# Two narrow score products as plain 32-bit products, and a later place for two kinds of VectorE work, in a hybrid encoder step

## The reference, cut to what matters

```python
def attend_block(q_nope, q_pe, q_chunk, k_nope, k_pe, v, k_chunk):
    s = jnp.einsum("bqhd,bkhd->bhqk", q_nope, k_nope) + jnp.einsum("bqhr,bkr->bhqk", q_pe, k_pe)
    s = s.astype(jnp.float32) * SM_SCALE
    mask = k_chunk[None, :] <= q_chunk[:, None]
    s = jnp.where(mask[None, None], s, -1e30)
    w = jax.nn.softmax(s, axis=-1).astype(v.dtype)
    return jnp.einsum("bhqk,bkhd->bqhd", w, v)
```

## Time and profile before

| what | value |
|---|---|
| median of 3 runs | 2449.06 us (2448.76 to 2449.34) |
| the profiled execution | 2446.93 us, of which its span 2445.1 |
| TensorE busy / weight loads | 99% / 96% of the span |
| VectorE, ScalarE, GpSimd busy | 74%, 52%, 22% |
| granted TensorE clock | 0.999 of full |

### The profile page before, as it was taken

One profiled execution on the slowest core, in us unless ns is written; L12 is line 12 of the kernel. 1 busy time (PEld: TensorE's weight loads), 2 busy tenths in 40 slices (PEclk: granted clock), 3 DMA queues, 4 the chain that ended last, 5 costly groups with the idle time before them and its releaser, 6 DMA issues. The chain is left out here.

```text
span 2445.1 us, 44182 instructions
## 1 busy us (share of the span) xinstructions
PE 2427.2 (99%) x17358; PEld 2340.8 (96%) x17358; DVE 1806.5 (74%) x2893; ACT 1283.4 (52%) x2306; POOL 537.9 (22%) x513
## 2 busy tenths in 40 slices
PE   9999999999999999999999999999999999999998
PEld 9999977899999999999999999778999999999998
DVE  8677767778776677677686777687787766776676
ACT  5566355655554454455535763557455544554454
POOL 0024155200112211220201142552002112211212
PEclk9999999999999999999999999999999999999999
DMA  4232200453447634664731221005435456546655
GB/s 164 71 115 73 53 11 20 88 154 106 96 86 139 129 84 98 133 120 90 221 100 52 61 73 54 11 20 115 133 109 114 88 115 132 109 87 121 132 104 185
DMA packets 109740, 242.48 MB, mean 99 GB/s; under 512 B 15536, under 2 KB 18960, under 8 KB 109408
## 3 DMA queue, kind: packets, MB, share of 16 engines
q0 software_dynamic: 48512, 102.26, 23.3%
q1 hardware_dynamic: 60880, 137.37, 18.0%
q10 hardware_dynamic: 144, 0.04, 0.0%
HBM read 147.39 MB, written 94.29 MB: 99 GB/s over the span
## 5 line engine op out<-in xcount | busy, mean ns | idle before, releaser
L3270 DVE TENSOR_TENSOR wlo<-raw_all,whi 128x512 fp32r<-128x512 f32 (+1 forms) x420 | 270.6, 653 | 181.1 <-ACT whi L2308 178.6
L2308 ACT ACTIVATE whi<-raw_all 128x512 fp32r<-128x512 f32 (+1 forms) x420 | 248.6, 599 | 278.4 <-DVE raw_all L3403 88.0
L3792 POOL DMA_DIRECT2D x_scratch<-stage x224 | 200.0, 943 | 839.1 <-DVE stage L3413 694.0
L2361 ACT ACTIVATE stage<-ps 128x536 f32<-128x536 f32 (+1 forms) x224 | 135.5, 612 | 148.6 <-PE ps L1590 143.6
L3413 DVE TENSOR_TENSOR stage<-stage,ps 128x536 f32<-128x536 f32 (+1 forms) x168 | 118.9, 708 | 84.8 <-PE ps L1590 84.0
L2873 DVE TENSOR_REDUCE mxp<-ps 128x1 f32<-128x80 f32 (+10 forms) x376 | 137.1, 376 | 51.7 <-PE ps L1304 47.7
L1113 PE MATMUL ps<-xgh,whi 128*128 128x358 f32 (+1 forms) x720 | 157.2, 326 | 0.0
L1113 PE MATMUL ps<-xgl,whi 128*128 128x358 f32 (+1 forms) x720 | 156.6, 325 | 0.0
L1113 PE MATMUL ps<-xgh,wlo 128*128 128x358 f32 (+1 forms) x720 | 156.5, 325 | 0.0
L1738 ACT ACTIVATE whi<-raw_all 128x1024 fp32r<-128x1024 f32 (+3 forms) x64 | 58.1, 908 | 174.5 <-PE ps L1113 158.0
L1113 PEld LDWEIGHTS ps<-xgl,whi 128*128 128x128 f32 x720 | 124.0, 189 | 0.0
(11 more groups left out here) (948 smaller groups left out, 7799.7 us busy)
## 6 DMA issues: line engine op xcount, KB each, us to landing
raw_all<-in_wst SPq DMA_DIRECT2D x237, 256.0 KB, 3.4
raw_all<-in_wst SPq DMA_DIRECT2D x74, 512.0 KB, 3.6
x_scratch<-stage POOLq DMA_DIRECT2D x120, 268.0 KB, 6.1
x_scratch<-stage POOLq DMA_DIRECT2D x120, 264.0 KB, 6.0
xall<-x_scratch SPq DMA_DIRECT2D x32, 537.0 KB, 8.6
x_scratch<-xall POOLq DMA_DIRECT2D x24, 537.0 KB, 3.5
raw_all<-in_wst POOLq DMA_DIRECT2D x30, 256.0 KB, 5.5
xall<-in_xT SPq DMA_DIRECT2D x8, 537.0 KB, 8.4
```

What stands on the lines that cost most here:

```text
L2308: nc.scalar.activation(dst, src, ACT.Copy).then_inc(S["u_hi"], 1)
L2361: nc.scalar.activation(quarters(stage_of(L, g, i, n)[:, 0:N2]), src, ACT.Copy, scale=-1.0 if row else 1.0).then_inc(S["x_copy"], 1)
L3270: V.tensor_tensor(dst, src, hi.bitcast(F32), ALU.subtract).then_inc(S["u_lo"], 1)
L3792: pool.dma_start(x_scr[2 * i + row, :, a:b], stage_of(L, g, i, n)[:, 0:b - a], accum_op=ALU.add).then_inc(S[done], 16)
```

## The change

- The scores of pairs 11 and 16 are made by one fp32 product each instead of three fp32r passes. Its operands are `q_plain` (the last 96 queries) and `k_plain` (the last 256 keys), which VectorE puts together from high and low parts in each head (`plain_parts`, two TENSOR_TENSOR, at step `PLAIN_AT` = 8). TensorE waits for them by the semaphore `plain`, which takes the place of `v_one`.
- `INVERT_AT` goes from 10 to 14.
- The copy of the sums of bank 1 goes from step 12 to step 13 (`SUM_LAG`).

```diff
+SUM_LAG = [OUT_LAG, OUT_LAG + 1, OUT_LAG]
-INVERT_AT = 10
+INVERT_AT = 14
+PLAIN = [PAIRS.index(SAMPLE_PAIR), PAIRS.index(LAST_PAIR)]
+PLAIN_AT = 8
+        q_plain = place("q_plain", "E", 2144 * 4, 64 + DEC)
+        k_plain = place("k_plain", "E", 2144 * 4 + 4 * (64 + DEC), 2 * P)
...
-                        for j, (a, c) in enumerate(PASSES):
+                        if i in PLAIN:
+                            w("plain", 1 + h + 1)
+                            mm = nc.tensor.matmul(ps[:, gi % 3, 0:n], k_plain[rows, k0 - LAST_KEYS:k0 - LAST_KEYS + P], q_plain[rows, q0 - STREAM + 64:q0 - STREAM + 64 + n],
+                                                  start=True, stop=True)
+                        for j, (a, c) in enumerate(() if i in PLAIN else PASSES):
...
+                def plain_parts(h):
+
+                    e = h % 2
+                    rows = slice(0, ALL_ROWS[e])
+                    w("aug", 32 * (h + 1))
+                    w("aug_few", 32 * (h + 1))
+                    w("q_lo", h + 1)
+                    if h == 0:
+                        w("kslot_lo", 1)
+                    else:
+                        w("kslot_lo", 4)
+                        w("s", h * NP)
+                    qh, ql = (qs[e][part][rows, STREAM - 64:TOK].bitcast(F32) for part in range(2))
+                    kh, kl = (ks[e][part][rows, LAST_KEYS:LAST_KEYS + 2 * P].bitcast(F32) for part in range(2))
+                    V.tensor_tensor(q_plain[rows, :], qh, ql, ALU.add)
+                    V.tensor_tensor(k_plain[rows, :], kh, kl, ALU.add).then_inc(S["plain"], 1)
...
+                        if i == PLAIN_AT:
+                            plain_parts(h)
...
-                            hb, ib = divmod(h * NP + i - OUT_LAG - BANK_LAST[n_bank], NP)
+                            hb, ib = divmod(h * NP + i - SUM_LAG[n_bank] - BANK_LAST[n_bank], NP)
```

More of the change, by code:

```diff
@@ L674, in trunk @@
             ("qr_raw", 2), ("qn", 4), ("qr", 2), ("ra0", 16 * 4), ("ra1", 16 * 4),
-            ("y_sq", 4), ("y_sum", 3), ("y_n", 4), ("v_one", 1), ("v_ev", 10), ("kf", 4),
+            ("y_sq", 4), ("y_sum", 3), ("y_n", 4), ("plain", 1 + NH), ("v_ev", 10), ("kf", 4),
             ("kslot_hi", 3), ("kslot_lo", 4),
@@ L2022, in o_out @@
                     nc.scalar.activation(d[r, q0:q1], ps[0:64, O_BANKS[n], 0:q1 - q0], ACT.Copy).then_inc(S["o_ev"], 1)
-                w("v_one", 1)
+                w("plain", 1)
                 for t in range(10):
@@ L2826, in _ @@
                     V.memset(kf[j][:, 3 * KCH:KW], 0.0)
-                V.memset(v[:, :].rearrange("p (t d) -> p t d", d=65)[:, :, 64:65], 1.0).then_inc(S["v_one"], 1)
+                V.memset(v[:, :].rearrange("p (t d) -> p t d", d=65)[:, :, 64:65], 1.0).then_inc(S["plain"], 1)
                 split(28)
```

## The result

The changed kernel takes **2470.37 us** (median of 5 runs, 2465.69 to 2473.74) against 2448.76 for the kernel before in the same comparison (5 runs, 2446.83 to 2449.34): ratio 1.0089, 95% interval 1.0075 to 1.0103. That is 21.6 us slower. I had forecast slower, but by 4.8 us, and the time lies above the top of the range. The profiled execution has a span of 2467.4 us.

A forecast was written before the change was run, and what follows sets the result against it. TensorE, busy 99% of the span, was taken to bound the kernel. The terms -3.5 - 7.5 + 10.1 + 4.5 + 1.2 gave +4.8 on the median 2449.06, so 2453.9 us, range 2447.0 to 2460.5.

The forecast's parts named there:

- the shifts of the few queries: Heads 3, 5, 7: GpSimd's small DMAs queue behind the reciprocals' store, TensorE waits 1.7 us six times: +10.1 us.
- The products: Pairs 11 and 16 on TensorE: one plain fp32 product saves 0.11 us over three passes: -3.5 us in all.
- The fifth rival: Pairs 11 and 16: fp32 weights load at half pace, adding time instead of saving: +7.0, 2460.9 us; 3%.
- The transposes: Attention stage: TensorE's 14 waits for VectorE's gathered maxima go, as copy and reciprocal move behind the gathering: -7.5 us.
- The third rival: Heads 3, 5, 7: `few_shifts` lands in time, its wait hidden; fully hidden -5.3, 2443.8 us; 12%.
- The new sums against GpSimd: Heads 0 and 4: GpSimd's low parts hold up VectorE's sums at step 8, so TensorE's maxima product waits: +4.5 us.
- rivals 1 and 2: VectorE's sums: not held by GpSimd, 2449.4 us, 15%; or GpSimd gets between head 0's two sums, 2459.8 us, 15%.
- the row at 221.52: GpSimd took 4.14 us while VectorE's sums ran, read as one side keeping the other out over several instructions.
- Head 7: Sums stand behind `yb20l`, so the 32-column product starts 0.9 us late, 0.3 comes back, in each layer: +1.2 us.
- The fourth rival: Attention stage: the transposes still wait because the sums are longer than thought: +7.5, 2461.4 us; 5%.
- The third step of the sum: Heads 3, 5, 7: delayed small DMAs of `few_shifts` taken to land in 1.6 us (1.5 to 2.2): +10.1 us.
- the forecast's own range: Whole kernel: 2451.5 to 2458 us, from the ends of the landing and of the products; the forecast had 50%.

The follow-up runs named there:

- the placed products alone: Changed kernel with both VectorE moves undone, GpSimd's queue as before, sums of head 0 at step 5 and head 7 at step 7: 2448.14 us, ratio 0.9997.
- the kernels with the exchange: `few_shifts` DMAs ahead of the reciprocals' store: changed kernel 2447.94 us; also sums of heads 0, 7 earlier 2443.68, 2442.89; without plain products 2443.98, 2444.37.
- the first five experiments: Reciprocals at step 10, 2451.25 us; GpSimd queue order, 2447.94; both VectorE moves without plain products, 2463.97; plain products without moves, 2454.76; head 5's weights later, 2459.88.
- everything placed: Changed kernel with `few_shifts` DMAs ahead of the reciprocals' store, sums of head 0 at step 5 and head 7 at step 7: 2443.68 us, again 2442.89.
- moves and exchange alone: Kernel before with both VectorE moves and `few_shifts` DMAs ahead of the reciprocals' store, without plain products and sums: 2443.98 us, again 2444.37.
- the moves alone: Kernel before with reciprocals at step 14 and the copy of bank 1 a step later, pairs by three passes, no sums: 2463.97 us, ratio 1.0064.

## Why the prediction was wrong

The term that failed is the third, the shifts of the few queries: its mechanism is the one that ran, but it measured 16.3 us and not 10.1. And the sum had no term for what long waits do to TensorE's clock, without a reason given; below it is estimated at 8.4 us. Term by term:

**The products (-3.5): right, a little too much.** Pair 11 of head 2, from the product of V ahead of it; the kernel before, then the changed one:
```profile
352.19 0.41 PE L1358 MATMUL ps<-pd,v 128*65 128x128 f32 x2
```
```profile
355.03 0.41 PE L1365 MATMUL ps<-pd,v 128*65 128x128 f32 x2
355.28 0.31 PE L1384 MATMUL ps<-q_plain,k_plain 97*128 97x32 f32 x2
355.42 0.48 PE L1311 MATMUL ps<-koh,qo 128*128 128x512 f32 x1
```
The plain product takes 0.14 us where I reckoned 0.22 to 0.26, 0.20 less than the three passes. But the product of V ahead of it, of type fp32 in both kernels, now takes 0.25 from start to start, not 0.17. The weight loads (engine PEld) show both at once; the kernel before, then the changed one:
```profile
352.33 0.30 PEld L1376 LDWEIGHTS ps<-qe,keh 97*128 97x128 f32 x2
352.67 0.19 PEld L1304 LDWEIGHTS ps<-koh,qo 128*128 128x128 f32 x1
```
```profile
355.17 0.30 PEld L1384 LDWEIGHTS ps<-q_plain,k_plain 97*128 97x128 f32 x2
355.40 0.19 PEld L1311 LDWEIGHTS ps<-koh,qo 128*128 128x128 f32 x1
```
From the first load of the pair to the next product's load it is 0.34 us for three passes and 0.23 for the plain product: two loads instead of three, 0.11 each, which is what I had reckoned. The first load stands under the product of V, so part of its time is booked there. In pair 16 I was off: its three passes take 0.40, so 96 columns do not quite fit under the same load. There the product goes from 0.40 to 0.19 and the one ahead from 0.19 to 0.33. Net 0.11 and 0.07, and 16 x 0.19 = 3.0 in all. The fifth rival (fp32 loads at half pace) is out. The Trainium skill (TensorE: Matmul & The Clock Gate, "Weight-path perf modes") would have fp32 weights without the fast load; here a load of the plain product is 0.19 us long and starts 0.11 behind the last, as a pass's does, so the trace does not show it slower than the passes.

Of the 3.0 about 1 remains. The kernel with the placed products alone shows where 2 go: the sums reach into the reductions. In head 4 `q_plain` takes 0.95 us instead of 0.25, until GpSimd's instruction ends at 390.37, and TensorE comes to its maxima product 0.27 later than without (0.38 in layer 1); in head 0 at step 5 another 0.3 to 0.4 us go in each layer, and the transposes of heads 2, 4, 6 wait 0.1 longer.

**The transposes (-7.5): right in place, in part given back.** In the changed kernel a transpose follows its product by 0.14 us where it was 0.92 in head 2. With nothing held behind the reciprocal, the moves brought 5.3 and 4.5 us of the 7.5. I booked all of it because a wait had gone; I looked for what would be late next only among the reductions. It is VectorE's copies of the next head's queries and keys (`qe<-ra`, `keh<-kf`), behind which the first maxima product now waits (1.5 to 1.8 us in all in the kernels with the exchange), and ScalarE's `pn` and the shifts of head 6, 0.3 to 0.7 each.

**The shifts of the few queries (+10.1): right mechanism, the step that was mis-sized.** It measured 14.9 us in the waits view, 16.3 by the spacing of starts. Heads 3 and 7 wait 2.06 and 1.86 in layer 0, near the 1.68; L3755 took 0.76 instead of 0.50 us to issue. But head 5 waits 3.9 and 4.0 us. I took the landing from a view of all issues (median 1.6, at most 2.2) and did not ask what else would be under way at the later moment. It was the one place where the moved DMAs fell together with 512 KB of weights. I had even written that SyncE's DMAs stay as they are; I did not ask whether the small ones would be moved onto them. Nor did head 3 of layer 1 keep to the median: its two landed in 2.1 and 2.2 us, and TensorE waited 2.5. The third rival (hidden) is out.

**The new sums against GpSimd (+4.5): right, with one step otherwise.** VectorE and GpSimd in head 0 of the changed kernel:
```profile
311.35 2.51 DVE L2939 TENSOR_TENSOR q_plain<-qe 97x96 f32<-97x96 f32 x1
313.79 0.41 DVE L2940 TENSOR_TENSOR k_plain<-keh,kel 97x256 f32<-97x256 f32 x1
```
```profile
311.27 2.48 POOL L3728 TENSOR_TENSOR qo<-ra,qo 32x1074 fp32r<-32x1074 f32 x1
313.81 3.18 POOL L3728 TENSOR_TENSOR kol<-kf,koh 64x1296 fp32r<-64x1296 f32 x1
```
The short sum lasts as long as GpSimd's instruction, and `k_plain` then gets between that and the next one, which takes 3.18 instead of 2.95. So rivals 1 and 2 are out. The waits are 2.0 and 1.8 us (2.1 and 1.8 forecast); those of head 4, forecast at 0.3 in either layer, are the 0.27 and 0.38 named above. Here the Trainium skill (SBUF — State Buffer, "SBUF: two separate sides"), by which the port is held for one whole instruction and no longer, was the better guide than the row at 221.52.

**Head 7 (+1.2): right mechanism.** TensorE came 0.80 and 0.77 us late at pair 11 (0.9 forecast, though its rows give 0.83); what the end of the head gives back was not separated.

**What was missing: the clock.** By the trace three falls cost 5.1 us in the profiled execution. Over the five runs the mean granted clock is 0.9956 for 0.999 before, and 0.0034 of 2468 us is 8.4; the clock is given to three digits, so this estimate is good to about 1 us. With it the medians nearly close: -3.0 - 7.3 + 16.3 + 3.8 + 1.6 + 8.4 is 19.8 of the 21.6, and the 1.8 left are of the size of the late work named above. (7.3 is the transposes' wait by spacing: 8 of 0.35 and 6 of 0.76.) In the profiled execution, which stands 22.5 above that of before, the same sum with 5.1 for the clock gives 16.5, and 3.3 are other waits (waits view above, lines of L1120, L1601, L1311 issue, L1365 and L1387 DMA, less 0.4 that L1120's place had before and 0.6 that another place, L1180, had more before); some 3 us stay unassigned.

The forecast missed by 16.8 us. 8.4 of it are the clock and 2 x 2.2 the landing in head 5 (3.9 for 1.7), three quarters together. The third step of the sum took a landing from a quiet place, and the sum had no term for what a long wait does to the rate of the work after it. The fourth rival (transposes still wait) is out as well. The lower end of the forecast's own range, 2451.5, does not follow from the ends that it names (the shortest landing gives 2453.3); the time lay far above it either way.

## What to carry to other kernels

When an instruction is moved later, list what stands behind its *consumers* in every queue, and let what does not need it go first: here exchanging two steps on GpSimd turned +21.6 us into -0.3, and with the sums placed clear of GpSimd's work into -5.6 and -5.9. Take the landing time of a delayed DMA from what is in flight at its new moment, not from the median of all its issues. Count a long wait of a busy TensorE dearer than its length: removing the queueing brought back the 16.3 us of waits and between 5 and 6 us more.

## What the runs showed of the hardware

**A wait of 2 us inside a dense stretch can bring the clock down.** In the profiled executions of the changed kernel and the first five experiments TensorE waited 28 times for 1.7 to 4.0 us at the places named. The granted clock fell after all four waits of 3.6 us or more; at six of the 24 of 1.7 to 2.5 us it did too (once before the wait ended). The same wait of 2.0 us in head 0 gave 0.83 in the changed kernel and 1.00 in the one with the reciprocals back at step 10:
```profile
310.00:320.00 10.00, 8.16 (x46) 6.25 (x46) 8.41 (x17) 3.45 (x15) 6.81 (x4) 1.00 0.01 2
```
So a wait of about 2 us did it in one execution and not in another, and what decides is not shown; after the four longest it came each time. Without such a wait it is all but absent: all 43 runs of the kernels with everything placed, and of moves and exchange alone, show 0.999, as do all 70 of the kernel before in the three comparisons; of the 11 runs of the placed products alone one shows 0.998. It also widens the spread, 2465.69 to 2473.74 in the changed kernel, at clocks of 0.997 to 0.994. That the wait is the cause rests on taking waits away; a wait of adjustable length at one place was not tried.

**Small DMAs of GpSimd beside a large one of SyncE** land in 3.4 to 3.8 us instead of 1.6, though the queues are different ones. This holds for head 5 in both layers of the changed kernel and of the moves alone, where SyncE's 512 KB were asked for 0.06 us after the first and some 0.45 us ahead of the second. In the kernel before they were asked for 0.3 us after the second, and both landed in 1.5 to 1.6. Moving the large one alone undid it (1.5 to 1.8).

**An fp32 product of 32 columns is two weight loads long.** Its loads start 0.11 us apart, as those of fp32r passes do, 0.23 us to the next product's load against 0.34 for three passes. In the matmul rows it looks shorter (0.14 for both records), and the fp32 product ahead of it 0.08 longer, 0.13 in front of 96 columns.

Why L3755 took 0.76 and 0.79 us to issue in heads 3 and 5 instead of 0.50 was not tried.
